# Decode scores and values of a paged attention layer written to four groups of 32 output partitions in turn

## The reference, cut to what matters

```
for each decode sequence b:                  # 8 of them
    pages = page_table[b]                    # 16 page numbers
    K, V  = cache_k[pages], cache_v[pages]   # 8 heads x 128 tokens x 128
    gate  = q . mean of K over blocks of 256 tokens -> the best 3 blocks per row
    p     = softmax(q.K * scale over these blocks, and q.k_new)
    out   = p.V + p_new.v_new
```

## Time and profile before

| what | us |
|---|---|
| time, median of 3 runs | 2848.68 (2845.56 to 2850.18) |
| span of the profiled execution, first to last instruction | 2843.8 |
| around the span, to the median | 4.9 |
| one scores turn (8 units, 16 pages), 166.54 to 220.39 | 53.85 |
| one values step (1 unit, 4 pages), 648.11 to 658.30 | 10.19 |
| values stage, 634.66 to 960.52 | 325.86 |

### The profile page before, as it was taken

How to read it: one execution, slowest core, us unless ns; L and a number is a source line. 1 busy time by engine, 2 the same in 40 slices (tenths; PEclk the granted TensorE clock), 3 DMA queues, 4 the chain that set the end, 5 groups by cost and what they waited for, 6 DMA issues and landing times.

```text
span 2843.8 us, 51136 instructions
## 1 busy us (share of the span) xinstructions
PE 2740.9 (96%) x19408; PEld 2416.9 (85%) x19408; DVE 1172.0 (41%) x1852; ACT 710.6 (25%) x1226; POOL 120.9 (4%) x265
## 2 busy tenths in 40 slices
PE   8999999979999999789999999999999999999994
PEld 8876767654444699789999999999999999999994
DVE  7433222340111433584343434444444343434357
ACT  5211111250111222342222222222222222222231
POOL 3000000000000000130000000000000000000002
PEclk9999999999999999899999999999999999999997
DMA  4455556407777442222222222222322223232321
GB/s 162 138 200 211 207 197 219 152 8 234 242 239 245 147 156 88 59 71 89 86 89 87 86 89 86 87 89 78 96 81 92 85 89 88 87 86 89 87 91 74
DMA packets 146616, 347.23 MB, mean 122 GB/s; under 512 B 16608, under 2 KB 16608, under 8 KB 146048
## 3 DMA queue, kind: packets, MB, share of 16 engines
q1 hardware_dynamic: 144480, 338.35, 37.2%
q0 software_dynamic: 2080, 8.14, 0.8%
HBM read 334.32 MB, written 12.10 MB: 122 GB/s over the span
## 4 chain that ended last, share of the span: by engine, by line
PE 93%; DVE 4%; DVEq 1%; ACT 1%; issue 0%; DMA 0%; POOL 0%; SPq 0%; ACTq 0%; POOLq 0%
PE ps_acc L705 28%; PE ps_acc L682 18%; PE ps_a L705 14%; PE ps_b L705 14%; PE ps_a L747 8%; PE ps_a L859 4%; PE ps_b L859 4%; PE ps_a L682 1%; PE ps_b L682 1%; PE ps_acc L801 1%; DVE act_lo L957 1%; DVE region L1362 0%; DVE w_lo L261 0%; DVE region L1247 0%; DVE region L1366 0%
## 5 line engine op out<-in xcount | busy, mean ns | idle before, releaser
L261 DVE TENSOR_TENSOR w_lo<-w_raw,w_hi 128x512 fp32r<-128x512 f32 x724 | 502.1, 705 | 1217.2 <-ACT w_hi L255 1214.2
L255 ACT ACTIVATE w_hi<-w_raw 128x512 fp32r<-128x512 f32 x724 | 445.5, 628 | 1397.7 <-PE ps_acc L682 475.9
L705 PE MATMUL ps_acc<-act_hi,w_hi 128*128 128x272 f32 x1472 | 308.4, 291 | 33.8 <-DVE act_lo L957 18.9
L705 PE MATMUL ps_acc<-act_lo,w_hi 128*128 128x272 f32 x1472 | 306.9, 290 | 0.0
L705 PE MATMUL ps_acc<-act_hi,w_lo 128*128 128x272 f32 x1472 | 304.8, 288 | 0.0
L682 PE MATMUL ps_acc<-act_hi,w_hi 128*128 128x272 f32 x1280 | 273.6, 295 | 2.0 <-DVE scratch L968 1.1
L682 PE MATMUL ps_acc<-act_hi,w_lo 128*128 128x272 f32 x1280 | 264.6, 288 | 0.0
L682 PE MATMUL ps_acc<-act_lo,w_hi 128*128 128x272 f32 x1280 | 263.9, 288 | 0.0
L705 PEld LDWEIGHTS ps_acc<-act_hi,w_hi 128*128 128x128 f32 x1472 | 232.5, 190 | 36.5 <-issue 22.1
L682 PEld LDWEIGHTS ps_acc<-act_hi,w_hi 128*128 128x128 f32 x1280 | 199.8, 188 | 49.7 <-issue 48.3
L747 PE MATMUL ps_a<-region,q_blk 128*32 128x256 f32 x1024 | 233.2, 382 | 2.3 <-ACT q_blk L423 2.3
(11 more groups left out here) (210 smaller groups left out, 3981.1 us busy)
## 6 DMA issues: line engine op xcount, KB each, us to landing
w_raw<-units SPq DMA_DIRECT2D x724, 256.0 KB, 2.6
region<-kcache SPq DMA_DIRECT2D x128, 512.0 KB, 4.2
region<-vcache SPq DMA_DIRECT2D x128, 512.0 KB, 4.5
region<-xT SPq DMA_DIRECT2D x8, 544.0 KB, 6.7
region<-xT SPq DMA_DIRECT2D x4, 1088.0 KB, 8.4
yT<-region SPq DMA_DIRECT2D x8, 544.0 KB, 2.7
ext_out<-region POOLq DMA_DIRECT2D x8, 339.5 KB, 4.5
kT_out<-scratch POOLq DMA_DIRECT2D x8, 272.0 KB, 5.8
```

The lines of the kernel that those rows point to most:

```text
L255: act.activation(w_hi[:, s], w_raw[:, s], ACT.Copy).then_inc(hi_ready, 1)
L261: dve.tensor_tensor(w_lo[:, s], w_raw[:, s], w_hi[:, s].bitcast(F32), ALU.subtract).then_inc(lo_ready, 1)
L705: mm = pe.matmul(banks(mt, odd)[:, n, 0:HN], w[:, s, i, cols], half(a[:, kt], n), start=kt == 0 and w is w_hi and a is hi, stop=kt == 2 * ...
```

## The change

The four quads of a sequence's pages, and in the values four sequences, write to partitions 0 to 31, 32 to 63, 64 to 95 and 96 to 127 of the same PSUM bank, one matmul after the other. The four page slots become two sets of four half pages (`[:, t, s, 512]`), of 2 KB per partition each. A round of scores is one set: four pages, four heads each, 16 matmuls of 128 columns. A step of values is one set: half of one page of each of four sequences, 4 matmuls of 512 columns, once behind each half of a unit (`both`). One copy on ACT then takes all 128 partitions where four took 32 each, and the block sums and maxima on DVE are spread back by small copies. The copy of probabilities to `p_seq` (L526) goes. The loop over the values on SP is written out. SP loads 16 page numbers at a time for the scores; for the values, where the four sequences' numbers don't lie side by side, it loads one number four times per unit.

```diff
-        pages = reg2[:, 8192:12288].rearrange("p (s n) -> p s n", s=RING)
+        pages = reg2[:, 8192:12288].rearrange("p (t s n) -> p t s n", t=SETS, s=4)
...
             with sp.Fori(4, 12) as g:
+                sp.load(pg, rows[bass.ds(g - 4, 1), :])
                 for u in range(8):
-                    if u % 4 == 0:
-                        sp.load(pg, table[bass.ds(2 * g - 8 + u // 4, 1), :])
                     load_unit(sp, 2 * g, u + RING)
-                    for i in (2 * u, 2 * u + 1):
-                        load_page(kcache, i % RING, pg[i % 8], 16 * g - 64 + i + 1)
-            with sp.Fori(12, 16) as g:
+                    sp.wait_ge(page_used, ROUNDS * g - 4 * ROUNDS + u + 1)
+                    for quad in range(4):
+                        load_half(kcache, u % SETS, quad, pg[4 * quad + u // 2], u % 2)
+            for j in range(4):
+                i, first = j // 2, 8 * (j % 2)
                 for u in range(8):
-                    if u % 2 == 0:
-                        sp.load(pg, table[bass.ds(4 * g - 48 + u // 2, 1), :])
-                    load_unit(sp, 2 * g, u + RING)
-                    for i in range(4 * u, 4 * u + 4):
-                        load_page(vcache, i % RING, pg[i % 8], 32 * g - 384 + 128 + i + 1)
+                    load_unit(sp, 24 + 2 * j, u + RING)
+                    for e in range(4):
+                        sp.load(vg[e:e + 1], table[8 * i + 2 * e + j % 2:8 * i + 2 * e + j % 2 + 1, u:u + 1])
+                    for part in range(2):
+                        sp.wait_ge(page_used, ROUNDS * DB + 16 * j + 2 * u + part + 1)
+                        for e in range(4):
+                            load_half(vcache, part, e, vg[e], part)
...
-                    for h in range(NH):
-                        mm = pe.matmul(ps_a[0:HC, quad % 2, s * P:(s + 2) * P], q_blk[:, h * HC:(h + 1) * HC],
-                                       pages[:, s:s + 2, h * P:(h + 1) * P], start=h == 0, stop=h == NH - 1)
-                    mm.then_inc(page_used, 2)
+                    for i in range(HALF):
+                        h = part * HALF + i
+                        for quad in range(4):
+                            mm = pe.matmul(ps_a[quad * HC:(quad + 1) * HC, 0, r * P:(r + 1) * P],
+                                           q_blk[:, h * HC:(h + 1) * HC], pages[:, t, quad, i * P:(i + 1) * P],
+                                           start=h == 0, stop=h == NH - 1)
+                    mm.then_inc(page_used, 1)
...
+            def values(i, pg, part):
+                o = (ps_a, ps_b)[i]
+                pe.wait_ge(page_loaded[part], 64 * (ROUNDS * DB // 2 + PAGES * i + pg + 1))
+                c = ((pg % 4) * 4 + pg // 4) * HC
+                for e in range(4):
+                    mm = pe.matmul(o[e * HC:(e + 1) * HC, part, :], s_all[:, 4 * i + e, c:c + HC],
+                                   pages[:, part, e], start=pg == 0, stop=pg == PAGES - 1)
+                mm.then_inc(page_used, 1)
...
             row_max(1)
+            for i, dst in enumerate((gate, bmax)):
+                for quad in range(4):
+                    dve.tensor_copy(dst[:, :, 2 * quad:2 * quad + 2], stat4[quad * HC:(quad + 1) * HC, i])
...
+            for e in range(4):
+                dve.tensor_copy(rinv4[e * HC:(e + 1) * HC], rinv.rearrange("p (i e) -> p e i", e=4)[:, e])
```

More of the change, by code:

```diff
@@ L58 @@
 LEAD = 3
+SETS = 2
+HALF = NH // 2
+ROUNDS = 8
 G_POOL = 16
@@ L154, in build @@
         rank = sb("rank", [HC, DB, NBLK])
+        stat4 = sb("stat4", [P, 2, DB, 2])
+        rinv4 = sb("rinv4", [P, 2])
         mx = sb("mx", [HC, 4, DB])
@@ L186, in build @@
         st_free = sem("st_free")
-        page_loaded = [sem(f"page_loaded{i}") for i in range(RING)]
+        page_loaded = [sem(f"page_loaded{i}") for i in range(SETS)]
         page_used = sem("page_used")
@@ L285, in _, with load_half @@
         def _(sp):
-            pg = [sp.alloc_register(f"page{i}") for i in range(8)]
+            pg = [sp.alloc_register(f"page{i}") for i in range(PAGES)]
+            vg = [sp.alloc_register(f"vpage{i}") for i in range(4)]
+            rows = table.rearrange("(b x) c -> b (x c)", x=2)
             def load_x(i):
                 sp.dma_start(x_in[:, 2 * i:2 * i + 2], xT[:, 2 * i:2 * i + 2]).then_inc(x_loaded[i], 16)
-            def load_page(cache, slot, reg, used):
-                if used is not None:
-                    sp.wait_ge(page_used, used)
+            def load_half(cache, t, slot, reg, part):
                 i = sp.snap(reg, min_val=0, max_val=N_PHYS - 1)
-                sp.dma_start(pages[:, slot], cache[bass.ds(i, 1)].rearrange("a p n -> p (a n)"))\
-                    .then_inc(page_loaded[slot], 16)
+                src = cache[bass.ds(i, 1)].rearrange("a p n -> p (a n)")[:, part * 512:(part + 1) * 512]
+                sp.dma_start(pages[:, t, slot], src).then_inc(page_loaded[t], 16)
             sp.dma_start(gain[:], gains).then_inc(const_in, 16)
@@ L424, in load_q, with store_scores @@
                     .then_inc(q_ready, 1)
[L426 to L430, removed]
+            def store_scores(b):
+                act.wait_ge(page_used, ROUNDS * b + ROUNDS + SETS)
+                act.activation(s_all[:, bass.ds(b, 1)].rearrange("p a n -> p (a n)"),
+                               ps_a[:, 0, :], ACT.Copy).then_inc(scores_out, 1)
             def kv_group(g):
@@ L444, in _ @@
                 kv_group(g)
-                store_scores(g - 4, 3)
+                store_scores(g - 4)
                 copy_heads(kT, 4, g)
@@ L513, in _, with store_values @@
             act.wait_ge(dve_s, 3)
-            def store_values(i, s):
+            def store_values(i):
                 act.wait_ge(hist_placed, 1)
[L518 to L530, removed]
+                act.wait_ge(page_used, ROUNDS * DB + 32 * (i + 1) + SETS)
+                act.activation(o_all[:, i], (ps_a, ps_b)[i][:, :, :].rearrange("p a n -> p (a n)"), ACT.Copy,
+                               scale=rinv4[:, i:i + 1]).then_inc(pv_out, 1)
+            for j in range(4):
+                for u in range(8):
+                    split_hi(act, 24 + 2 * j, u + LEAD)
+                if j % 2:
+                    store_values(j // 2)
             def pool_hi(j):
@@ L664, in _, with group @@
         def _(pe):
-            def group(G, q, nu, hi, lo, ready=None, after=None, k0=0, first=False, odd=0, units=None, prev=1):
+            def group(G, q, nu, hi, lo, ready=None, after=None, k0=0, first=False, odd=0, units=None, prev=1, both=False):
                 for u in units or range(nu):
@@ L686, in group @@
                             mm.then_inc(acc_done, 1)
+                        if both and mt == 0:
+                            after(u, 0)
                     mm.then_inc(unit_used, 1)
-                    if after is not None:
+                    if both:
+                        after(u, 1)
+                    elif after is not None:
                         after(u)
@@ L844, in _ @@
             pe.wait_ge(pa_stored, NH)
[L847 to L864, removed]
+            def values(i, pg, part):
[6 more added lines that the diff above has]
+                mm.then_inc(page_used, 1)
+            for j in range(4):
+                group(12 + j, 24 + 2 * j, 8, act_hi, act_lo,
+                      after=lambda u, part, i=j // 2, p0=8 * (j % 2): values(i, p0 + u, part), both=True)
             def own_rows(a):
@@ L873, in own_rows @@
                 return mm
-            pe.wait_ge(pv_out, DB + 1)
+            pe.wait_ge(pv_out, 1)
             own_rows(0)
@@ L1017, in _, with block_stats @@
             heads(3, 6, odd=1)
[L1019 to L1025, removed]
+            def block_stats(b):
+                dve.wait_ge(scores_out, b + 2)
+                src = s_all[:, bass.ds(b, 1)].rearrange("p a (k n) -> p (a k) n", k=2)
+                for i, op in enumerate((ALU.add, ALU.max)):
+                    dve.tensor_reduce(stat4[:, i, bass.ds(b, 1)].rearrange("p a k -> p (a k)"), src, AX.X, op)
             def kv_splits(g):
@@ L1037, in _ @@
                 heads(g, 2 * g)
-                block_stats(g - 4, 3)
+                block_stats(g - 4)
             with dve.Fori(8, 12) as g:
```

35 lines of the change are left out of this document (13 added, 22 removed).

## The result

The changed kernel takes 2781.14 us (median; 2775.01 to 2784.32), the one before 2849.43 us beside it on the same chip: a ratio of 0.9761, 95% interval 0.9747 to 0.9775. The profiled span went from 2843.8 to 2779.0 us, 64.8 less. The forecast was 2766.

What follows compares the result with a forecast made beforehand. PE, busy 96% of the span, was taken to bound the kernel. From the span of 2843.8, -98 for scores, +14 for values and +1.4 for DVE gave 2761, plus 4.9 to the median: 2766 us, range 2665 to 2950.

Steps and rivals of the forecast that it cites:

- The scores term: Scores stage on PE: a turn falls from 53.85 to 40.1 us, 1.5 charged for late sets, 98 us less over eight turns.
- I take half, 1.73 us: Scores on PE: a round of 32 instructions takes 1.73 us, half of 3.45, as partition groups overlap only in part.
- the 1.25: Scores on PE: lower bound of a round, 32 instructions at 39 ns each, taken from 16 small instructions' starts.
- wrong in kind: Sign of failure: PE waits over 3 us a scores turn for pages, or a low clock makes PE's work set the values step.
- The values term: Values stage: SP's loads and issues set a step of 10.9 us, 340 us for 325.9, 14 us more.
- L = 6.7 us: Values on SP: time of a step's four pairs of page-number loads, at 1.67 us a pair.
- The middle of the least price: Values on SP: each pair of loads priced by values read, (2.57 + 0.77)/2 = 1.67 us.
- Rival B: Values on SP: loads cost by the load, 3.16 us a pair, step 16.8 us, +191 us, total 2943; chance 0.24.
- The clock: Values on PE: half rate after waits adds 2.5 us to PE's 6.9, still under the 10.9 us step; nothing charged.
- DVE's copies: Before the ranking of blocks: eight small copies on DVE, on which PE waits, add 1.4 us.
- A: Scores on PE: partition groups don't overlap, so scores gain nothing; total 2870 us, slower; chance 0.18.
- C: Values: loads go by values, DMA sets an 8 us step, -74 us; total about 2660, faster; chance 0.23.

## Why the prediction was right, and where it was not

The direction held, and the time was 15 us off. But that closeness is luck: two errors of opposite sign nearly cancel. From the forecast's span of 2761: -33 for the scores, +48 for the values, +3 for the rest, 2779.

**The scores term failed in the step "I take half, 1.73 us: of two instructions on the same partitions the second must follow the first, and only it can overlap the next group's first".** The first half of that sentence is true (109 ns from one to the next in a group); the second is not. In the interleaved order all four groups run at once, and a round is 1.01 us, under the 1.25 that I had drawn as a floor from the starts of 16 small instructions. The order decides: group by group the same round is 2.39. A turn is 297.5/8 = 37.2 us, in the 36 to 38 that the prediction gave to four groups.

Summed from the starts of PE's instructions and its idle time before them, the stage of 428.8 us was 199.5 in units and 229.3 in page matmuls; the 297.5 of now are 205.0 in units, 67.9 in page matmuls and 24.6 of waits. So the page matmuls won 161 us where the sum had 110, the late sets took 25 where it had 12, and another 5.5 went into the units, for which it had no term: -161.4 + 24.6 + 5.5 = -131.3. I had named waits of more than 3 us a turn as a sign of being wrong in kind; 24.3/8 = 3.04 stands just over that bound. They come with the shorter round, since the same bytes have to pass in less time: DMA is at 0.87 of a stage that holds these waits.

The Trainium skill ("TensorE: Matmul & The Clock Gate", Part 3) measured a factor of 2.38 for three column groups. Here four groups gave 3.57/1.01 = 3.5 and two at a time 3.57/1.47 = 2.4, each with the turn from unit to page work in it. The same section has matmuls start and end strictly in program order; by that a block of one group could overlap the next with its last instruction alone, about 0.1 us. The group-by-group round speaks for 0.4, so the measurement and that rule differ here.

**The values term failed in its size, not its mechanism.** SP's own step became the bound, with PE waiting in every step, as said. I took L = 6.7 us for four pairs; it is 7.7 as the mean of the two gaps shown, and of all 30. "The middle of the least price" for each pair is not how it is made up: in the first gap the first pair took 692.99 - 689.08 = 3.9 us and the three others 697.32 - 692.99 = 4.3; in the second gap the first took 704.69 - 702.27 = 2.4 and the others 4.7. So one pair costs 3.2 and each other 1.5. Eight half pages took 4.1 to 4.3 us, not 3.68. Together 1.5 us a step, and 30 x 1.52 = 46 of the 48 us missed. Rival B's price (every pair 3.16) was wrong by the same trace; its turning point, a step of 13.6 us, lay close above the 12.42 measured. The kernel whose pairs read eight numbers shows how close: its four times 0.42 us a step ate nearly all of the gain.

The Trainium skill's 200 ns per register ("Runtime: NRT & Kernel Launch", Instruction fetch mechanics) would have made eight numbers 1.4 us dearer than one. Measured is 0.42.

**The clock.** In the values, waits of 5 to 6 us put PE's matmuls at the lower level afterwards (granted clock 0.78 over the stage), and SP's step covered it: charged nothing, cost nothing. In the scores, where PE holds most of the chain, nothing was charged either, and there it shows: behind late sets the granted clock fell (0.58 and 0.72 in the stretches above), four of the eight late rounds were 0.2 to 0.7 us longer, and the units 5.5 us in all. How much of that would have come back as waits for keys at the full clock is not shown.

**DVE's copies.** The stretch in which they stand grew by 2.4 us where 1.4 was charged. What the other microsecond is was not taken apart.

**The rivals.** A (no overlap) is excluded by the round, C (about 2660, with half overlap or with four groups) was right where it took four groups, with a turn near 37 us, and wrong in its loads. Once the loads are taken away the kernel does what C said: 2671.74, with DMA busy 0.84 of the values stage.

## What to carry to other kernels

Work that leaves the bound engine is won only as far as the next one in line allows: here a matmul change was paid for by a scalar load on the queue that feeds it, and mending that load was worth more (109 us) than the change had been (68 us). Before a change spreads one long transfer over many short ones, count what the issuing queue does for each of them, above all the first load behind issued transfers. Where several partition groups of PE are to work at once, alternate them instruction by instruction, and then look at once at whether the data keeps up.

## What the runs showed of the hardware that was not expected

- Float32 matmuls of 32 stationary columns in four partition groups: 1.01 us for 32 instructions in alternation, 1.47 with two groups at a time, 2.39 one group after the other.
- A load into SP's registers: 0.46 us for one page number, 0.88 for eight, 1.67 for sixteen; 0.82 for an address of two values, and 1.2 to 3.8 us for the address load right behind issued transfers.
- PE behind a wait of 2.23 us in the scores: a granted clock of 0.58 in the round that follows, and 0.72 in the 3.5 us after it. Of the eight late rounds, behind waits of 1.7 to 3.2 us, four were no longer than the others.
- Transfers of 2 KB rows ran at 273 to 291 GB/s with a DMA share of 0.84 to 0.87, in the scores and, once SP no longer held them up, in the values.
